# A macaron block's hand-overs by token tile, and 64x64 products in its block inversion

## The reference, cut to what matters

```python
h = layer_norm(DEEPNORM_ALPHA * h + 0.5 * swiglu(h, ffn1_w_gate[l], ffn1_w_up[l], ffn1_w_down[l]),
               ln1_g[l], ln1_b[l])
mix = hybrid_mixer(h, w_in[l], ...)
h = layer_norm(DEEPNORM_ALPHA * h + mix, ln2_g[l], ln2_b[l])
h = layer_norm(DEEPNORM_ALPHA * h + 0.5 * swiglu(h, ffn2_w_gate[l], ffn2_w_up[l], ffn2_w_down[l]),
               ln3_g[l], ln3_b[l])
```

```python
a_mat = jnp.where(strict, jnp.einsum('bhncd,bhned->bhnce', k_beta, k) * decay, 0.0)
m_mat = a_mat + jnp.eye(CHUNK, dtype=a_mat.dtype)
value = solve(v_beta)
k_cumdecay = solve(k_beta * jnp.exp(g_cum)[..., None])
```

## Time and profile before

| | us |
|---|---|
| median of 3 runs | 2034.58 |
| lowest and highest | 2033.61, 2034.80 |
| the profiled execution's own time | 2034.15 |
| its span, first to last instruction | 2032.4 |
| PE busy | 1987.6 (98%) |
| DVE busy | 1100.6 (54%) |
| ACT busy | 849.9 (42%) |
| DMA queue of the weights | 54.7% of 16 engines' span |

### The profile page before, as it was taken

The page is one execution under the profiler, slowest core; times in us unless marked ns, Lnnn a source line. Parts: engine busy times, 40 slices in busy tenths (PEclk is TensorE's granted clock), DMA queues, the critical chain, the costliest instruction groups (busy, mean ns, idle before and its releaser), DMA issues.

```text
span 2032.4 us, 27995 instructions
## 1 busy us (share of the span) xinstructions
PE 1987.6 (98%) x10219; PEld 1693.8 (83%) x10219; DVE 1100.6 (54%) x1239; ACT 849.9 (42%) x953; POOL 83.9 (4%) x101
## 2 busy tenths in 40 slices
PE   9999999999999999999988999999999999999996
PEld 7888888888888879999988977788888888888885
DVE  4555555555444555777585365755554555544455
ACT  4444444444333334445554533344444444433342
POOL 0000000000000011000033300000000000000000
PEclk9999999999999999999999999999999999999998
DMA  8666656665556666564520027466666666655663
GB/s 279 189 189 192 186 176 188 202 188 188 170 190 206 207 177 200 179 188 124 175 92 1 1 94 268 155 189 191 189 186 186 184 197 187 191 170 188 204 200 121
DMA packets 186085, 355.02 MB, mean 175 GB/s; under 512 B 11201, under 2 KB 24097, under 8 KB 185265
## 3 DMA queue, kind: packets, MB, share of 16 engines
q1 hardware_dynamic: 184224, 345.29, 54.7%
q0 software_dynamic: 1696, 8.99, 1.4%
q10 hardware_dynamic: 112, 0.05, 0.0%
HBM read 352.18 MB, written 2.10 MB: 174 GB/s over the span
## 4 chain that ended last, share of the span: by engine, by line
PE 91%; DVE 4%; issue 3%; ACT 1%; POOL 0%; DMA 0%; DVEq 0%; SPq 0%; POOLq 0%; ACTq 0%
PE acc L338 26%; PE acc L340 25%; PE acc L339 25%; PE acc L349 3%; PE acc L353 3%; PE acc L351 3%; PE tp L568 1%; PE acc L1756 1%; PE tp L1743 1%; PE tp L387 1%; DVE resid L675 0%; DVE resid L470 0%; DVE wlo L319 0%; PE acc L397 0%; ACT whi L313 0%
## 5 line engine op out<-in xcount | busy, mean ns | idle before, releaser
L319 DVE TENSOR_TENSOR wlo<-raw,whi 128x1024 fp32r<-128x1024 f32 (+2 forms) x667 | 797.3, 1203 | 821.4 <-ACT whi L313 821.4
L313 ACT ACTIVATE whi<-raw 128x1024 fp32r<-128x1024 f32 (+2 forms) x667 | 690.0, 1042 | 1011.3 <-PE acc L340 932.3
L338 PE MATMUL acc<-whi,xT 128*128 128x512 f32 (+2 forms) x1724 | 662.1, 384 | 5.0 <-DVE xT L440 2.8
L340 PE MATMUL acc<-whi,xT 128*128 128x512 f32 (+2 forms) x1724 | 657.6, 381 | 0.0
L339 PE MATMUL acc<-wlo,xT 128*128 128x512 f32 (+2 forms) x1724 | 657.0, 381 | 0.0
L338 PEld LDWEIGHTS acc<-whi,xT 128*128 128x128 f32 x1724 | 324.3, 188 | 74.6 <-DVE xT L440 3.3
L340 PEld LDWEIGHTS acc<-whi,xT 128*128 128x128 f32 x1724 | 324.2, 188 | 62.0
L339 PEld LDWEIGHTS acc<-wlo,xT 128*128 128x128 f32 x1724 | 324.4, 188 | 58.3
L338 PE MATMUL acc<-whi,hT 128*128 128x512 f32 x704 | 275.3, 391 | 1.9 <-DVE resid L675 1.9
L340 PE MATMUL acc<-whi,hT 128*128 128x512 f32 x704 | 274.2, 389 | 0.0
L339 PE MATMUL acc<-wlo,hT 128*128 128x512 f32 x704 | 274.0, 389 | 0.0
(11 more groups left out here) (297 smaller groups left out, 1124.3 us busy)
## 6 DMA issues: line engine op xcount, KB each, us to landing
raw<-in_ffn_w_up_dram SPq DMA_DIRECT2D x176, 512.0 KB, 3.7
raw<-in_ffn_w_down_dram SPq DMA_DIRECT2D x176, 512.0 KB, 4.3
raw<-in_ffn_w_gate_dram SPq DMA_DIRECT2D x175, 512.0 KB, 3.7
raw<-in_w_in_dram SPq DMA_DIRECT2D x48, 512.0 KB, 3.6
raw<-in_w_out_dram SPq DMA_DIRECT2D x32, 512.0 KB, 6.8
raw<-in_w_in_dram SPq DMA_DIRECT2D x32, 260.0 KB, 2.8
raw<-in_w_in_dram SPq DMA_DIRECT2D x16, 456.0 KB, 4.1
raw<-in_w_q_idx_dram SPq DMA_DIRECT2D x8, 512.0 KB, 6.0
```

What stands on the lines that cost most here:

```text
L313: act.activation(whi[:, s, :, 0:w], raw[:, r, :, 0:w], ACT.Copy).then_inc(hi_done, 1)
L319: dve.tensor_tensor(wlo[:, s, :, 0:w], raw[:, r, :, 0:w], whi[:, s, :, 0:w].bitcast(F32), ALU.subtract).then_inc(lo_done, 1)
L338: pe.matmul(o, hi, whi[:, s, k, 0:width], start=first and k == 0, stop=False)
L340: ins = pe.matmul(o, lo, whi[:, s, k, 0:width], start=False, stop=last and k == UNIT_KT - 1)
```

## The change

It has two parts.

**Hand-overs by token tile.** In the last chunk of `F1D`, `WO` and `F2D` the last three units are multiplied for the first tile, all three, and then for the second (`exit_units`). Their split weights go to six additional slots, `edge_hi` and `edge_lo`, so that the three `whi` slots can already take the next phase's first three units. The norm is worked out tile by tile: `exit_tiles` does the first tile's sum, statistics, variance and first quarter ahead of the second tile's sum. `tile_to_xT_*` transposes and splits 512 columns of one tile at a time, and `entry_units` multiplies the next phase's first eight units by half units in an order that follows these. There are 6 filling matmuls where there were 22. At the end `exit_tiles` with `LAST_ORDER` normalises all of the first tile's quarters but starts two of them ahead of the second tile's sum, and SP stores in the same order.

**64x64 products.** In steps 0 to 19 of the inversion each 128x128 product becomes two 64x64 products of the diagonal quarters, and the transpositions of steps 0 to 15 become ordinary products with the identity, two 64x64 ones for each 128x128 transposition.

```diff
-START_WAIT, NORM_WAIT, SOFTMAX_WAIT = 6, 22, 24
+START_WAIT, NORM_WAIT, SOFTMAX_WAIT = 6, 6, 24
...
+        edge_hi = mz("edge_hi", 16, [P, STAGGER, UNIT_KT, BANK], F32R)
+        edge_lo = mz("edge_lo", 28, [P, STAGGER, UNIT_KT, BANK], F32R)
...
+        def exit_units(pe, p, stat):
+
+            n, it = st.phases[p].units, st.phases[p].iters - 1
+            for half in range(2):
+                for u in range(n - STAGGER, n):
+                    if half == 0:
+                        pe.wait_ge(lo_done, st.index(p, it, u + 1))
+                    ins = token_mm(pe, p, it, u, acc0, half, stat, 2 * u, False, u == n - 1)
+                    if half == 1:
+                        ins.then_inc(unit_used, 1)
+                if half == 0:
+                    ins.then_inc(acc0a_done, 1)
...
+        def entry_units(pe, e, p, n_chunk):
...
+            tile_to_xT_pe(pe, e, 0, 0)
+            keep_warm(pe, p, tp[:, 3], NORM_WAIT)
+            half_unit(0, 0)
+            tile_to_xT_pe(pe, e, 0, 1)
+            half_unit(1, 0)
+            for q in range(OUT_CHUNKS):
+                if q > 0:
+                    half_unit(2 * q, 0)
+                    half_unit(2 * q + 1, 0)
+                if q < OUT_CHUNKS - 1:
+                    tile_to_xT_pe(pe, e, q + 1, 0)
+                half_unit(2 * q, 1)
+                half_unit(2 * q + 1, 1)
+                if q < OUT_CHUNKS - 1:
+                    tile_to_xT_pe(pe, e, q + 1, 1)
...
+        NORM_ORDER = [(0, 0), (1, 0), (0, 1), (1, 1), (2, 0), (2, 1), (3, 0), (3, 1)]
+        LAST_ORDER = [(0, 0), (1, 0), (2, 0), (3, 0), (0, 1), (1, 1), (2, 1), (3, 1)]
...
+        def exit_tiles(dve, e, p, scale):
+
+            c = OUT_CHUNKS - 1
+            resid_tile(dve, p, c, scale, KU if p == WO else DOWN_U, 0)
+            norm_variance(dve, e, 0)
+            norm_tile(dve, e, 0, 0)
+            if e == 2:
+                norm_tile(dve, e, 1, 0)
+            resid_tile(dve, p, c, scale, KU if p == WO else DOWN_U, 1)
+            if e < 2:
+                tile_to_xT_dve(dve, e + 1, 0, 0)
+            norm_variance(dve, e, 1)
+            if e < 2:
+                norm_tile(dve, e, 1, 0)
+            else:
+                for q, t in LAST_ORDER[2:]:
+                    norm_tile(dve, e, q, t)
...
                         if s < JOIN:
-                            ins = pe.matmul(bankF(s % 4)[:, k * P:k * P + P], lev[:, t, h], xinv[:, t, h],
-                                            start=True, stop=True)
+                            for rows in CHUNKS:
+                                cols = slice(k * P + rows.start, k * P + rows.stop)
+                                ins = pe.matmul(bankF(s % 4)[rows, cols], lev[rows, t, h, rows], xinv[rows, t, h, rows],
+                                                start=True, stop=True)
...
                         if s - 2 < JOIN - 4:
-                            ins = pe.transpose(bankF(n)[:, k * P:k * P + P], yinv[:, t, G8 * hh + k], ident[:])
+                            for rows in CHUNKS:
+                                cols = slice(k * P + rows.start, k * P + rows.stop)
+                                ins = pe.matmul(bankF(n)[rows, cols], yinv[rows, t, G8 * hh + k, rows],
+                                                ident[rows, rows], start=True, stop=True)
```

349 lines of the change are left out of this document (212 added, 137 removed).

## The result

| | before | after |
|---|---|---|
| median, us | 2034.5 (4 runs) | 2011.7 (4 runs) |
| lowest and highest | 2033.61, 2034.80 | 2011.17, 2012.85 |
| ratio of the times | | 0.9889, 95% interval 0.9872 to 0.9907 |
| the profiled execution's own time | 2034.15 | 2011.17 |
| its span | 2032.4 | 2009.4 |

The account below looks back on a forecast made before the run. PE was taken as the bound, 91% of the chain that ended last. Savings of 3.9 + 2.9 + 3.9 + 2.0 + 11.1 = 23.8 us from 2034.15 gave 2010.35, stated as 2010.5 us; range 2005 to 2022.

Parts of the forecast that it names:

- the end: Last norm behind PE's last product: the first tile's norm starts earlier, last instruction ends at 2027.6, not 2029.62; 2.0 us gained.
- steps 4 to 19: Inversion: overlapping 64x64 quarters bring a step from 2.22 to 1.65 us; 15 steps save 8.6 us.
- second gap: Hand-overs: PE finishes six products, then waits for the second tile's norm before its transpositions; 1.9 to 2.6 us lost.
- the half units don't hide the norm: Rival, hand-overs: later half DVE-bound, 14 norm tiles each leave 0.3 us uncovered, 4 us given back, 2014.5; chance 0.07.
- the clock falls again: Rival, hand-overs: two shorter stretches with little work in each still lower PE's clock; costs 2.9 us, 2013.4; chance 0.25.
- 2.9, since the longest stretch with little work shrinks: F1D to WA: PE's longest stretch shrinks from 3.9 to about 2.2 us, clock stays at 2.4 GHz; 2.9 us gained.
- the reading of 0.036 us a pass as the rate at which PE's queue is supplied: Inversion: joining steps' 0.29 us per 8 passes taken as queue supply, 1.74 us a step, so 1.65 forecast.
- ACT's two copies of 0.5: Inversion: ACT's work in a step, counted as two copies of 0.5 us, below the forecast step of 1.65.
- Who is late next?: Inversion: POOL's 1.27, DVE's 0.69 or 1.38 and ACT's copies all stay below 1.65 us a step.
- The first rival: Inversion: two quarters writing one PSUM bank take turns, a step costs 2.74 us, time 2029.3; chance 0.13.
- PE's part of steps 2 and 3 gets shorter by some 1.3: Inversion ahead of step 4: DVE sets the pace, but PE's shorter work there gains some 1.3 us.
- The rival with a fallen clock in the inversion: Half-filled array drops the clock to 1.2 GHz: 2070 us without overlap, chance 0.03; 2029 with overlap, chance 0.02.

Follow-up runs that it names:

- blocked kernel: The changed kernel with each inversion operation's upper quarters all issued before its lower ones, same instructions; 2015.44 us, ratio 0.9915.
- filled kernel: The changed kernel with 8, 7 and 3 filling matmuls ahead of the first products of inversion steps 1, 2 and 3; 2006.99 us, ratio 0.9864.

## Why the prediction was right, step by step

**The sum.** 23.8 was forecast from the profiled execution and 23.0 came. The terms were less exact than that:

| term | forecast | measured |
|---|---|---|
| hand-over F1D to WA | 3.9 + 2.9 for the clock | 5.1 |
| hand-over WO to F2GU | 3.9 | 4.1 |
| the end | 2.0 | 1.5 |
| lead-in of the inversion | 1.3 | 0.0 |
| steps 4 to 19 | 8.6 | 9.9 |
| behind step 19 | 1.2 | 1.7 |
| places that the change leaves alone | 0 | 0.7 |

**Hand-overs.** The gap ahead of the first half unit was 2.49, forecast 2.4: the count of DVE's steps from the first tile's sum to its norm held to 0.3 us. The second gap was 1.85 long at WO (1.69 of it a plain wait) and 2.0 at WA, at the lower end of 1.9 to 2.6. POOL's power was hidden, as the step said. The rival that the half units don't hide the norm is out: with 4.1 gained nothing was given back.

**The clock at WA.** In this profile half of the rival "the clock falls again" came true. It fell in the second gap, but for 3.4 us instead of 6.8. Half clock takes half of the time away, so the remaining loss is some 1.7, and 3.9 + 2.9 - 1.7 = 5.1, as measured. In the ten other profiles with this hand-over and its fillings it didn't fall, and there the stretch from F1D's last product to WB is 48.47 to 48.70 us against 55.41 before: 6.7 in those with the same order, the forecast 6.8. So the step "2.9, since the longest stretch with little work shrinks" held in ten profiles of eleven, and the result's own profile is the eleventh.

**Steps.** Here the step that failed is the reading of 0.036 us a pass as the rate at which PE's queue is supplied. The blocked kernel has the same 0.036 with the same number of instructions, and the alternating one has 0.029: it was the order of the quarters that limited the joining steps, where the other quarter's product came in the queue only now and then. What I took for the supply, and added to the floor of 1.37, isn't there. Measured steps are 1.40 where nobody is late, close to that floor. The average from step 4 to step 19 is (1138.78 - 1115.31)/15 = 1.56, and 1.51 in the kernel with the filled lead-in ((1135.56 - 1112.91)/15). Of the 2.5 us above 15 steps of 1.40, 1.05 is step 4 at half clock. Four steps from 1119.16 to 1125.09 take 1.45 to 1.50, 0.3 in sum, and there ACT is the one that is late:

```profile
1120.00:1122.00 2.00, 2.00 (x74) 1.98 (x70) 0.83 (x2) 2.00 (x6) 1.83 (x2) 1.00 0.00 0
```

It has three instructions a step there, one every 0.5 us and busy for all of the 2.00: besides the two copies that "ACT's two copies of 0.5" counted, it makes `thz_sb` (L1255). The other 1.1 is DVE, in four steps from 1130.69 to 1137.41, 1.67 to 1.69 each. It scales `zab` in eight steps, which I had at 1.38 (two instructions of 0.69); in the first four it only uses up its lead. In the kernel before each `zab` instruction fell between two of POOL's:

```profile
1139.18 0.68 DVE L1474 SCALAR_TENSOR_TENSOR zab<-thz_sb,zab 128x512 f32<-128x512 f32 x1
```

In the changed kernel POOL has hardly a pause and they run side by side:

```profile
1125.82 9.87 POOL L1047 TENSOR_TENSOR lev<-aT,pair_mask 128x512 f32<-128x512 f32 x6 [0.22 <-PE tp L1892]
...
1132.36 0.63 PE L1892 MATMUL tp<-xinv,lev 64*64 64x64 f32 x16
...
1132.80 0.67 DVE L1612 TENSOR_TENSOR yinv<-yinv,acc 128x512 f32<-128x512 f32 x1
...
1133.40 1.16 DVE L1629 TENSOR_TENSOR zab<-zab,og 128x512 f32<-128x512 f32 x1
...
1134.05 0.63 PE L1892 MATMUL tp<-xinv,lev 64*64 64x64 f32 x16
```

POOL now takes 9.87/6 = 1.64 an instruction, DVE 1.16 on `zab`, and DVE goes from one instruction to the next without idle time; the step is 1134.05 - 1132.36 = 1.69. From 1131 to 1136 DVE sets the pace in the steps that PE could do in 1.40. The Trainium skill, "SBUF — State Buffer", section "SBUF: two separate sides", names a pair of ports that GpSimd and a VectorE instruction with two SBUF inputs can't hold together, each for its whole length. Which instructions are hit agrees: `yinv`, with one input in PSUM, stays at 0.67. Whole lengths in turn would need 1.27 + 0.68 = 1.95 a step, and the step takes 1.69, so to that length the trace doesn't bear it out; by what each takes from start to start without the other (0.60 and 1.24) it would be 1.84, still more than 1.69, and how exact POOL's records are the trace doesn't say. "Who is late next?" was asked with durations from steps slow enough for the two engines to keep out of each other's way. The lead-in of the kernel before had them side by side already:

```profile
1107.73 1.77 POOL L899 TENSOR_TENSOR lev<-aT,pair_mask 128x512 f32<-128x512 f32 x1 [1.82 <-DVE aT L1440]
...
1108.41 1.64 DVE L1452 TENSOR_TENSOR yinv<-ident,yinv 128x512 f32<-128x512 f32 x1
```

So the row that would have warned was there. The forecast of 1.65 was 0.1 above the average of 1.56, and that nearness is luck: a supply limit that doesn't exist was put in, and the limits by DVE and ACT and the half clock at step 4, which do exist, were left out. The bounds beside it were mis-added too: 15 x (2.22 - 1.85) + 1.3 + 1.2 is 8.1, not 7.6, and with 1.4 it is 14.8, not 14.5. Neither changes the forecast or the range.

**The pairs in one bank.** The first rival is refuted: 16 passes of alternating quarters in 0.47 us, into one bank of `tp` or `acc`, against 16 x 0.057 = 0.91 one after the other. The Trainium skill, "TensorEngine Tiling (Array Packing)", section "Restrictions and Gotchas", forbids different row tiles the same PSUM bank at once. This case's trace doesn't agree for two quarters that write different partitions: the measurement decides.

**Lead-in.** The step "PE's part of steps 2 and 3 gets shorter by some 1.3" was right about the work: with the clock held up it is 1.7 (13.17 in the kernel before against 11.49). What it left out is that a shorter PE part between DVE's unchanged ones means more idle PE, and the clock takes that back. The rival with a fallen clock in the inversion named the wrong cause, an array half filled, and looked for evidence in the joining steps, which have no gaps; steps 4 to 19 of the filled kernel, quarters alone at 1.00, refute that cause. With step 4 the fall cost 2.8 us in this profile. The place where PE isn't the bound was the one to look at.

**The end.** 0.45 of the missing 0.5 us is the norm tile's size. Six tiles took 2006.63 - 1997.84 = 8.79, 1.465 each, not 1.39: a tile's two instructions take 0.78 and 0.67 from start to start. In the earlier trace rows the same instruction on two tiles stands side by side, 1.33 for the two, so the wait of the second instruction for the first, on the same tile, doesn't show there.

**The terms together.** The inversion is 0.5 above its forecast (-1.3, +1.3, +0.5), the first hand-over 1.7 below, the second 0.2 above, the end 0.5 below, and 0.7 came from elsewhere. These cancel to -0.8, so the sum was better than its terms.

## What to carry to other kernels

Where a change makes PE's part shorter in a stage that another engine paces, price the idle time that it leaves: here it cost the whole gain of the lead-in until eighteen filling matmuls brought it back, and such fillings cost nothing here as long as they ended before what PE waited for. Products on the two diagonal 64x64 quarters should be issued in turn, quarter by quarter, not block by block. For "who is late next", count every instruction that an engine has in a step, and ask whether the engines that were in turn before will now run side by side, since their durations then grow; and take a rate only from rows issued in the same order as the one to come. Where pieces are worth 1 or 2 us in 2000, measure the stretch between two marks in the trace: it repeated to 0.2 us where the clock did the same, while the runs of one kernel spread over up to 4.6.
